# Stick-breaking attention: log-sums over softplus kept per key tile, in two rounded matmul passes

## The chip, the core and the metric

The kernel runs on one core of one Trainium2 chip. The metric is the device time of one execution in microseconds (us). A chip's core has five engines that run side by side, each with its own queue in program order: TensorE (matmuls), VectorE, ScalarE, GpSimd, and SyncE, which issues the DMAs. They wait for one another through semaphores. In profile rows they are PE (PEld for its weight loads), DVE, ACT, POOL and SP.

## The reference

Two transformer-like blocks for 512 tokens of width 1024, in fp32. The first block has two layers, each a gated feed-forward network, a mixing stage, a second feed-forward network and a gated embedding; the second block has one layer with another mixer. The change is in the mixing stage of the first block, which adds up three branches: stick-breaking attention (4 heads of 64), latent attention (8 heads, softmax) and a short gated convolution. For queries t and keys s the stick-breaking branch is

```
z = q @ k.T * 64 ** -0.5                  # mask: s < t
log_not = where(mask, -softplus(z), 0)
after = reverse_cumsum(log_not over s) - log_not
w = where(mask, exp(log_sigmoid(z) + after), 0)
out = w @ v
```

As log_sigmoid(z) = z - softplus(z), the exponent is z minus the sum of softplus over the key itself and all later keys that the query may see.

## The kernel before

Activations lie as [features on 128 partitions, 512 tokens]. Eleven stages follow one another (ffn, mix, ffn, ple, twice; then mix2, ffn, ple). A product with weights is made exact enough by splitting both operands: ScalarE writes a copy rounded to the type F32R (the high part), VectorE subtracts it from the exact value (the low part), and TensorE adds three rounded matmuls (`trio`, L569). TensorE takes a rounded matmul in one pass, and an exact F32 one as two recorded half-passes, each itself two passes. Weights come from HBM by SyncE's DMAs into `raw`, are split by `split_high` (ScalarE, L442) and `split_low` (VectorE, L448), and SyncE issues the DMA of a unit once the low part of the unit two before it is done (L492).

The attention of a mixing stage (`tensor_attention` L961, `scalar_attention` L1551, `vector_attention` L2294) is an order written out by hand on each engine; nothing is reordered at run time. Three strands are woven together: projections of the latent branch; 16 latent steps (`score(t)`, `lat_exp(t)`, `divide(t)`, `turn(t)`, each of two heads and a query tile); and 8 rounds of the stick-breaking branch. A round r covers a pair of heads and one key tile j, from the last tile (3) down to 0, so the queries from tile j on, n = 4 - j tiles of 128 columns. Both heads stand in PSUM banks 4 and 5, which all rounds share. The steps of a round:

- `logits(r)` (TensorE, L1069): z, after the exponential of the round before has left the banks.
- `softplus(r)` (ScalarE, L1602): |z|, exp(-|z|), ln(1 + ...) into `TZ`.
- `masked(r)` (VectorE, L2340): `SP` = max(z, 0) + `TZ`; then the diagonal block is multiplied by the mask; then the diagonal block is copied to the running sum `SS`, if j > 0.
- `after_sum(r)` (TensorE, L1083): adds -1 (lower triangle `ntri`) times `SP` of the own tile, and -1 (`nones`) times `SS`, the running sum of all later tiles, for the queries beyond the own tile. Both are exact F32 matmuls. Then a bf16 matmul adds the mask.
- `weights(r)` (ScalarE, L1606): the exponential out of PSUM.
- GpSimd (L2646 to L2653) adds `SP` to `SS` for the columns beyond the diagonal, after `after_sum(r)`.

`lat_exp(t)` waits for `score_max(t)` on VectorE, `score(t + 1)` on TensorE waits for `lat_exp(t)`, `turn(t)` for `divide(t)`. `keep` (L1611, L2370) brings a finished head pair out of PSUM, again as high and low parts. After `lat_values(3)` the output projection begins (`tensor_last_rows`), with 192 matmuls over 8 units of weights. The first rows of it need the kept pairs.

The tiles of the attention lie in a region of 96 KB, `hid_at`, whose parts are used again and again. `SP` is one [128, 2, 512] tile and `SS` another. The functions that the change touches:

Of the kernel before, what the change touches and what calls it, by code (L numbers as in the profile page):

```python
# [15 lines left out]
P = 128  # L16
# [191 lines left out]
def build_program(nc, a, out):  # L208
    with ExitStack() as ctx:
        def sem(name, step=1):  # L210
            return Signal(ctx.enter_context(nc.semaphore(name)), step)

        cursor = [16 * KB + 128]

# [40 lines left out]
        masks = sb("masks", [P, 3, P], BF16)  # L255
        fw_cols = sb("fw_cols", [P, 4, 2])

        ident = consts[:, 0:P]
# [12 lines left out]
        def hid_tile(name, shape, kb, dt=F32):  # L271
            return at(name, shape, dt, hid_at + kb * KB)
# [21 lines left out]
        SW_FIRST = at("SW_FIRST", [P, 2, DC, T], F32, halves_at)  # L294
        SP = hid_tile("SP", [P, 2, T], 88)
        SS = hid_tile("SS", [P, 2, T], 92)
        PB = [R, RP, U[0], U[1]]
# [663 lines left out]
        def tensor_attention(e, s):  # L961
# [121 lines left out]
            def after_sum(r):  # L1083

                j = key_tile(r)
                rest = slice((j + 1) * P, T)
                e.wait_ge(*vec.at("sb_masked", s, r))
                for h in range(2):
                    e.matmul(ps[4 + h][:, j * P:T], ntri, SP[:, h, j * P:T], start=False, stop=False, skip_group_check=True)  # L1089
                if j < TC - 1:  # L1090
                    e.wait_ge(*(pool if j < TC - 2 else vec).at("sb_running", s, r - 1))
                    for h in range(2):
                        e.matmul(ps[4 + h][:, rest], nones, SS[:, h, rest], start=False, stop=False, skip_group_check=True)  # L1093
                for h in range(2):
# [456 lines left out]
        def scalar_attention(e, s):  # L1551
# [65 lines left out]
            softplus(0)  # L1617
            q_rope(0)
            q_rope(1)
            weights(0)  # L1620
            split_high(e, W[s, "key"])
            softplus(1)
            split_high(e, W[s, "value"])
            q_nope(0)
            weights(1)
            q_nope(1)
            softplus(2)
            key(1)
            key(3)
            lat_exp(0)  # L1630
            weights(2)
# [4 lines left out]
            log_part(3)  # L1636
            lat_exp(2)
            split_high(e, W[s, "out", 0])
            value(2)
# [3 lines left out]
            softplus(4)  # L1643
            value(3)
            lat_exp(5)
            weights(4)
            lat_exp(6)
            softplus(5)
            keep(7, "sb_values", 0, 0)
            lat_exp(7)  # L1650
            keep(6, "lat_values", 0, 2 + 0)
            split_high(e, W[s, "out", 1])
# [3 lines left out]
            softplus(6)  # L1656
            lat_exp(10)
            split_high(e, W[s, "out", 2])
            keep(6, "lat_values", 1, 2 + 1)
# [4 lines left out]
            softplus(7)  # L1664
            lat_exp(14)
            keep(6, "lat_values", 2, 2 + 2)
            lat_exp(15)
# [626 lines left out]
        def vector_attention(e, s):  # L2294
# [45 lines left out]
            def masked(r):  # L2340
                j = key_tile(r)
                diag = slice(j * P, (j + 1) * P)
# [7 lines left out]
                stt(e, SP[:, :, j * P:T], banks[:, 4:6, j * P:T], 0.0, TZ[:, :, j * P:T], ALU.max, ALU.add  # L2350
                    ).then_inc(*vec.done(("sb_softplus", s, r)))
                e.wait_ge(*vec.at("sb_softplus", s, r))
                e.tensor_tensor(SP[:, :, diag], SP[:, :, diag], mask01.unsqueeze(1).to_broadcast([P, 2, P]), ALU.mult
                                ).then_inc(*vec.done(("sb_masked", s, r)))
# [21 lines left out]
            conv_low(1)  # L2376
            masked(0)
            q_rotated(0)
            masked(1)
            split_low(e, W[s, "key"])  # L2380
            q_rotated(1)
            q_cos(0)
# [8 lines left out]
            masked(2)  # L2391
            score_max(0)
            score_max(1)
            divide(0)
# [4 lines left out]
            masked(3)  # L2399
            score_max(3)  # L2400
            divide(2)
            divide(3)
# [3 lines left out]
            masked(4)  # L2406
            turned(3)
            divide(4)
            score_max(6)
# [6 lines left out]
            masked(5)  # L2416
            score_max(8)
            divide(7)
            turned(6)
# [6 lines left out]
            masked(6)  # L2426
            turned(8)
            split_low(e, W[s, "out", 1])
            score_max(11)
# [15 lines left out]
            masked(7)  # L2445
            score_max(15)
            keep(6, 2 + 2)
            turned(14)
# [189 lines left out]
        def gpsimd_mix(e, s):  # L2638
# [6 lines left out]
            e.tensor_tensor(CS[:, 3, :], CS[:, 3, :], CS[:, 4, :], ALU.add).then_inc(*pool.done(("kv_squares", s)))  # L2645
            for r in range(ROUNDS):  # L2646
                j = key_tile(r)
# [129 lines left out]
```

## Time and profile before

| | us |
|---|---|
| median of 3 runs | 2835.51 (2834.59 to 2835.59) |
| span of the profiled execution | 2832.4 |
| around the span, by the median | 3.1 |
| TensorE busy | 2824.2 (100%), 14154 matmul records |
| VectorE busy | 1554.6 (55%), 2272 instructions |
| ScalarE busy | 1163.4 (41%), 1816 instructions |
| GpSimd busy | 36.6 (1%), 38 instructions |

The profiled execution's time is given as its span, from the first to the last instruction; the 3.1 us beside it are the difference to the median of the runs. Busy time is the union of an engine's records. Matmuls are pipelined and their ends are modelled, so records overlap and TensorE counts as busy where it only finishes; the distance between the starts of neighbours is the better price of a matmul. The clock granted to TensorE is full in every slice of the span.

### The profile page before, as it was taken

To read this page: it belongs to the slowest core of one execution; us is meant where nothing else is said; L and a number is where in the kernel's file an instruction comes from. 1 tells how busy PE (TensorE), PEld (TensorE's weight loads), DVE (VectorE), ACT (ScalarE), POOL (GpSimd) and SP (SyncE) were. 2 spreads that over 40 slices of the span, in tenths; PEclk is the share of its full clock that TensorE was granted. 3 is DMA by queue.
4 is the path that set the end of the run, shared out by engine and by line. 5 is a ranking of instruction groups with operands and counts; after the bars stand their busy time and mean duration, and the time that the engine had idled before them with its cause. 6 is when DMAs were issued, how large, how long until landed. Compare 5 with 4: busy or idle time off the path is not lost.

```text
span 2832.4 us, 35135 instructions
## 1 busy us (share of the span) xinstructions
PE 2824.2 (100%) x14154; PEld 2357.8 (83%) x14154; DVE 1554.6 (55%) x2272; ACT 1163.4 (41%) x1816; POOL 36.6 (1%) x38
## 2 busy tenths in 40 slices
PE   9999999999999999999999999999999999999999
PEld 7888887698888898888976788888987889888888
DVE  5443466755442585442566564433776756766437
ACT  5332344553332563332535543323754545322235
POOL 0000000000000000000000000000001100000000
PEclk9999999999999999999999999999999999999999
DMA  5333323033333223333232223333232323333331
GB/s 161 98 97 101 124 56 95 17 97 112 97 97 97 82 90 104 97 97 97 76 105 53 90 81 97 98 97 120 68 101 82 96 78 102 101 101 97 104 119 60
DMA packets 200657, 264.93 MB, mean 94 GB/s; under 512 B 34992, under 2 KB 153136, under 8 KB 200496
## 3 DMA queue, kind: packets, MB, share of 16 engines
q1 hardware_dynamic: 200352, 262.68, 30.4%
q8 instruction: 113, 1.85, 0.3%
q14 instruction: 48, 0.39, 0.0%
q10 hardware_dynamic: 144, 0.00, 0.0%
HBM read 258.44 MB, written 2.10 MB: 92 GB/s over the span
## 4 chain that ended last, share of the span: by engine, by line
PE 98%; DVE 1%; ACT 0%; issue 0%; DMA 0%; SPq 0%; DVEq 0%; ACTq 0%
PE banks L570 31%; PE banks L571 31%; PE banks L572 31%; PE banks L1030 1%; PE banks L1052 1%; PE banks L1089 1%; PE banks L1041 1%; PE banks L1093 0%; PE banks L1079 0%; PE banks L609 0%; PE banks L1183 0%; DVE PT L2366 0%; PE banks L1012 0%; PE banks L976 0%; PE banks L1014 0%
## 5 line engine op out<-in xcount | busy, mean ns | idle before, releaser
L570 PE MATMUL banks<-HH,WH 128*128 128x512 f32 (+1 forms) x3132 | 1140.1, 364 | 0.3 <-DVE HL L1790 0.3
L571 PE MATMUL banks<-HH,WL 128*128 128x512 f32 (+1 forms) x3132 | 1135.2, 362 | 0.0
L572 PE MATMUL banks<-HL,WH 128*128 128x512 f32 (+1 forms) x3132 | 1135.0, 362 | 0.0
L451 DVE TENSOR_TENSOR WL<-raw,WH 128x1024 fp32r<-128x1024 f32 (+1 forms) x482 | 581.5, 1209 | 981.4 <-ACT WH L446 981.0
L446 ACT ACTIVATE WH<-raw 128x1024 fp32r<-128x1024 f32 (+1 forms) x482 | 501.8, 1044 | 1012.0 <-PE banks L572 799.4
L570 PEld LDWEIGHTS banks<-HH,WH 128*128 128x128 f32 x3132 | 591.2, 189 | 100.7 <-issue 6.9
L572 PEld LDWEIGHTS banks<-HL,WH 128*128 128x128 f32 x3132 | 591.3, 189 | 91.9
L571 PEld LDWEIGHTS banks<-HH,WL 128*128 128x128 f32 x3132 | 591.4, 189 | 91.1 <-issue 1.0
L570 PE MATMUL banks<-HIDH,WH 128*128 128x512 f32 (+1 forms) x1056 | 377.7, 358 | 0.0
L572 PE MATMUL banks<-HIDL,WH 128*128 128x512 f32 (+1 forms) x1056 | 376.8, 357 | 0.0
L571 PE MATMUL banks<-HIDH,WL 128*128 128x512 f32 (+1 forms) x1056 | 376.8, 357 | 0.0
L571 PEld LDWEIGHTS banks<-HIDH,WL 128*128 128x128 f32 x1056 | 199.5, 189 | 29.2
L572 PEld LDWEIGHTS banks<-HIDL,WH 128*128 128x128 f32 x1056 | 199.5, 189 | 28.8
L570 PEld LDWEIGHTS banks<-HIDH,WH 128*128 128x128 f32 x1056 | 199.5, 189 | 28.7
L1427 ACT ACTIVATE HIDH<-U 128x512 fp32r<-128x512 f32 x112 | 69.3, 634 | 106.1 <-DVE U L2015 106.1
L1284 ACT ACTIVATE HH<-X,par 128x256 fp32r<-128x256 f32 x160 | 72.8, 502 | 85.5 <-DVE X L1910 85.5
L1423 ACT ACTIVATE G<-G 128x512 f32<-128x512 f32 x88 | 55.7, 632 | 124.3 <-DVE G L1982 124.3
L1982 DVE TENSOR_TENSOR U<-banks,R 128x512 f32<-128x512 f32 x112 | 76.6, 684 | 27.5 <-ACT G L1423 26.6
L1982 DVE TENSOR_TENSOR G<-banks,R 128x512 f32<-128x512 f32 x112 | 76.8, 686 | 18.1 <-PE banks L572 18.1
L1890 DVE TENSOR_TENSOR U<-U,SQY 128x256 f32<-128x256 f32 x120 | 50.8, 423 | 65.4 <-ACT SQY L1267 63.6
L2020 DVE TENSOR_TENSOR HIDL<-U,HIDH 128x512 fp32r<-128x512 f32 x112 | 72.6, 690 | 5.5
L1790 DVE SCALAR_TENSOR_TENSOR HL<-X,par,HH 128x256 fp32r<-128x256 f32 x160 | 70.0, 480 | 0.6 <-ACT HH L1284 0.6
(272 smaller groups left out, 1967.1 us busy)
## 6 DMA issues: line engine op xcount, KB each, us to landing
raw<-in_w_up SPq DMA_DIRECT2D x264, 256.0 KB, 3.1
raw<-in_w_down SPq DMA_DIRECT2D x112, 512.0 KB, 3.5
raw<-in_w_gate SPq DMA_DIRECT2D x168, 256.0 KB, 2.8
raw<-in_w_in SPq DMA_DIRECT2D x68, 512.0 KB, 3.7
raw<-in_w_ple_gate SPq DMA_DIRECT2D x24, 512.0 KB, 3.6
raw<-in_w_out SPq DMA_DIRECT2D x16, 512.0 KB, 3.8
raw<-in_w_rg_out SPq DMA_DIRECT2D x8, 512.0 KB, 3.5
raw<-in_w_o SPq DMA_DIRECT2D x8, 512.0 KB, 3.5
```

Source lines behind the costliest of these rows:

```text
L446: e.activation(WH[tile_of[u]][:, 0:n], raw[raw_of(u)][:, 0:n], ACT.Copy).then_inc(*high.done((u,)))
L451: e.tensor_tensor(WL[tile_of[u]][:, 0:n], raw[raw_of(u)][:, 0:n], WH[tile_of[u]][:, 0:n].bitcast(F32), ALU.subtract).then_inc(*low.done((u,)))
L570: e.matmul(o, wh, ah, start=start, stop=False, skip_group_check=skip)
L571: e.matmul(o, wl, ah, start=False, stop=False, skip_group_check=skip)
L572: return e.matmul(o, wh, al, start=False, stop=stop, skip_group_check=skip)
L1284: e.activation(HH[:, n, part(h)], X[:, n, part(h)], ACT.Copy, scale=pre_gain(s, n)).then_inc(*act.done(("h_high", s, h, n)))
L1423: e.activation(G[j][:], G[j][:], ACT.Silu).then_inc(*act.done(("gate", s, g, j)))
L1427: e.activation(HIDH[:, 2 * g + j, :], U[j][:], ACT.Copy).then_inc(*act.done(("hidden_high", s, 2 * g + j)))
L1790: return e.scalar_tensor_tensor(out=o, in0=in0, scalar=scalar, in1=in1, op0=op0, op1=op1)
L1890: e.tensor_tensor(TOTAL_Y[h], TOTAL_Y[h], SQY[y_place[s, h, n] % 2][:], ALU.add).then_inc(*vec.done(("y_sum", s, h, n)))
L1982: return e.tensor_tensor(o, ps[bank][:], R[:], ALU.mult).then_inc(*vec.done(event))
L2020: e.tensor_tensor(HIDL[:, k, :], U[j][:], HIDH[:, k, :].bitcast(F32), ALU.subtract).then_inc(*vec.done(("hidden_low", s, k)))
```

## The change

The softplus of each key tile is kept in a tile of its own until the pair of heads is done, split into a rounded high part `SPH[j]` (ScalarE, `sums_high`) and a rounded low part `SPL[j]` (VectorE, `sums_low`, in place of `SP[j]`). TensorE sums over tiles: for every tile later than j it adds `round_nones` times high and low, and for the own tile `round_ntri` times high and low. The running sum `SS`, its copy on VectorE, the additions on GpSimd and the waits for them are gone. Two 128x128 constants are rounded once at the start by ScalarE. The tiles are placed anew: the allocation begins 15 KB lower, and the scratch area for dynamic DMAs is set to 1 KB.

```diff
-        cursor = [16 * KB + 128]
+        cursor = [KB + 128]
...
+        round_nones = sb("round_nones", [P, P], F32R)
+        round_ntri = at("round_ntri", [P, P], F32R, consts_at + 4 * 6 * P)
+        SPH = [sb(f"SPH{j}", [P, 2, (TC - j) * P], F32R) for j in range(TC)]
+        widest_sp = take(4 * KB)
...
-        SP = hid_tile("SP", [P, 2, T], 88)
-        SS = hid_tile("SS", [P, 2, T], 92)
+        sp_at = [widest_sp, hid_at + 91 * KB, hid_at + 89 * KB, hid_at + 88 * KB]
+        SP = [at(f"SP{j}", [P, 2, (TC - j) * P], F32, sp_at[j]) for j in range(TC)]
+        SPL = [at(f"SPL{j}", [P, 2, (TC - j) * P], F32R, sp_at[j]) for j in range(TC)]
...
             def after_sum(r):
                 j = key_tile(r)
-                rest = slice((j + 1) * P, T)
-                e.wait_ge(*vec.at("sb_masked", s, r))
+                if r == 0:
+                    e.wait_ge(*act.at("round_sums", 1))
+                e.wait_ge(*vec.at("sb_softplus", s, r))
+                for earlier in range(TC - 1, j, -1):
+                    for h in range(2):
+                        for half in (SPH, SPL):
+                            e.matmul(ps[4 + h][:, earlier * P:T], round_nones[:], half[earlier][:, h, :], start=False,
+                                     stop=False, skip_group_check=True)
+                e.wait_ge(*vec.at("sb_low", s, r))
                 for h in range(2):
-                    e.matmul(ps[4 + h][:, j * P:T], ntri, SP[:, h, j * P:T], start=False, stop=False, skip_group_check=True)
-                if j < TC - 1:
-                    e.wait_ge(*(pool if j < TC - 2 else vec).at("sb_running", s, r - 1))
-                    for h in range(2):
-                        e.matmul(ps[4 + h][:, rest], nones, SS[:, h, rest], start=False, stop=False, skip_group_check=True)
+                    for half in (SPH, SPL):
+                        e.matmul(ps[4 + h][:, j * P:T], round_ntri[:], half[j][:, h, :], start=False, stop=False,
+                                 skip_group_check=True)
...
+            for i, (rounded, exact) in enumerate(((round_ntri, ntri), (round_nones, nones))):
+                e.activation(rounded[:], exact, ACT.Copy).then_inc(*act.done(("round_sums", i)))
...
+            def sums_high(r):
+                j = key_tile(r)
+                e.wait_ge(*vec.at("sb_masked", s, r))
+                e.activation(SPH[j][:], SP[j][:], ACT.Copy).then_inc(*act.done(("sb_high", s, r)))
...
             def masked(r):
...
-                    if key_tile(r - 1) > 0:
-                        e.wait_ge(*vec.at("sb_running", s, r - 1))
-                    if 0 < key_tile(r - 1) < TC - 1:
-                        e.wait_ge(*pool.at("sb_running", s, r - 1))
...
-                if j > 0:
-                    e.wait_ge(*vec.at("sb_masked", s, r))
-                    e.tensor_copy(SS[:, :, diag], SP[:, :, diag]).then_inc(*vec.done(("sb_running", s, r)))
+            def sums_low(r):
+                j = key_tile(r)
+                e.wait_ge(*act.at("sb_high", s, r))
+                e.tensor_tensor(SPL[j][:], SP[j][:], SPH[j][:].bitcast(F32), ALU.subtract).then_inc(*vec.done(
+                    ("sb_low", s, r)))
...
-                if 0 < j < TC - 1:
-                    rest = slice((j + 1) * P, T)
-                    e.wait_ge(*vec.at("sb_running", s, r))
-                    e.wait_ge(*pe.at("sb_sum", s, r))
-                    e.tensor_tensor(SS[:, :, rest], SS[:, :, rest], SP[:, :, rest], ALU.add
-                                    ).then_inc(*pool.done(("sb_running", s, r)))
```

The new calls stand in the written orders as follows. On ScalarE: `sums_high(0)` between `q_rope(0)` and `q_rope(1)`; (1) after `split_high` of "value", before `q_nope(0)`; (2) after `key(3)`, before `lat_exp(0)`; (3) after `lat_exp(2)`, before the split of output unit 0; (4) after `value(3)`, before `lat_exp(5)`; (5) after `lat_exp(7)`, before `keep(6, ...)`, the split of output unit 1 and `lat_exp(8)`; (6) after `lat_exp(10)`, before the split of output unit 2; (7) after `lat_exp(14)`, before `keep(6, ...)` and `lat_exp(15)`. On VectorE: `sums_low(0)` after `masked(0)`; (1) after the split of "key"; (2) after `score_max(0)`; (3) after `score_max(3)`, before `divide(2)`; (4) after `turned(3)`, before `divide(4)`; (5) after `score_max(8)`, before `divide(7)`; (6) after `turned(8)`, before the split of output unit 1 and `score_max(11)`; (7) after `score_max(15)`, before `keep(6, ...)`, `turned(14)` and `divide(15)`.

## Rows read from the trace of the kernel before

**Rows 1.** The page: busy us (share of the span) xinstructions of each engine.

```profile
PE 2824.2 (100%) x14154; PEld 2357.8 (83%) x14154; DVE 1554.6 (55%) x2272; ACT 1163.4 (41%) x1816; POOL 36.6 (1%) x38
```

**Rows 2.** Windows: us, then busy us (xinstructions) of each engine, clock, DMA.

```profile
468.20:561.70 93.50, 92.00 (x484) 58.96 (x482) 68.37 (x144) 57.51 (x123) 4.01 (x4) 1.00 0.14 39
533.20:547.20 14.00, 13.29 (x73) 7.86 (x70) 13.60 (x33) 9.05 (x22) 1.27 (x1) 1.00 0.13 39
```

**Rows 3.** Timeline of TensorE, start us then duration: rounded matmuls, first and last of a run.

```profile
401.06 0.39 PE L570 MATMUL banks<-HH,WH 128*128 128x512 f32 x1
...
404.91 0.39 PE L572 MATMUL banks<-HL,WH 128*128 128x512 f32 x1
...
583.68 0.28 PE L571 MATMUL banks<-HH,WL 128*128 128x256 f32 x1
...
588.12 0.28 PE L572 MATMUL banks<-HL,WH 128*128 128x256 f32 x1
...
2826.22 0.27 PE L571 MATMUL banks<-HH,WL 128*128 128x128 f32 x1
...
2828.68 0.28 PE L572 MATMUL banks<-HL,WH 128*128 128x128 f32 x1
```

**Rows 4.** Timeline of TensorE: the sums of rounds 1, 2 and 3.

```profile
484.27 1.02 PE L1089 MATMUL banks<-SP,consts 128*128 128x256 f32 x4
...
485.58 0.28 PE L1095 MATMUL banks<-masks 128*128 128x128 bf16 x2
...
494.53 1.51 PE L1089 MATMUL banks<-SP,consts 128*128 128x384 f32 x4
...
496.74 0.28 PE L1095 MATMUL banks<-masks 128*128 128x128 bf16 x2
...
507.38 1.94 PE L1089 MATMUL banks<-SP,consts 128*128 128x512 f32 x4
...
510.44 0.28 PE L1095 MATMUL banks<-masks 128*128 128x128 bf16 x2
```

**Rows 5.** Timeline: the mask of round 2, a weight split on ScalarE.

```profile
493.55 0.42 DVE L2353 TENSOR_TENSOR SP<-SP,consts 128x256 f32<-128x256 f32 x1
...
504.43 1.05 ACT L446 ACTIVATE WH<-raw 128x1024 fp32r<-128x1024 f32 x1
```

**Rows 6.** Timeline of VectorE: the score maximum of latent step 3.

```profile
507.58 1.23 DVE L2328 TENSOR_REDUCE stats<-banks 128x2 f32<-128x1024 f32 x1 [1.16 <-PE banks L1031]
```

**Rows 7.** Timeline, round 4: exponential of step 5, mask, score of step 6.

```profile
515.36 0.47 ACT L1585 ACTIVATE U<-banks,stats 128x256 f32<-128x256 f32 x1 [1.01 <-DVE stats L2328]
...
515.69 0.42 DVE L2353 TENSOR_TENSOR SP<-SP,consts 128x256 f32<-128x256 f32 x1
...
516.83 0.91 PE L1030 MATMUL banks<-KM,QM 96*128 96x384 f32 x2
```

**Rows 8.** Timeline, round 5: kept copy, mask, exponential of step 8, score of step 9.

```profile
525.78 0.59 ACT L1613 ACTIVATE HH<-banks 128x512 fp32r<-128x512 f32 x1
...
526.17 0.42 DVE L2353 TENSOR_TENSOR SP<-SP,consts 128x256 f32<-128x256 f32 x1
...
527.36 0.37 ACT L1585 ACTIVATE R<-banks,stats 128x128 f32<-128x128 f32 x1
...
528.18 0.65 PE L1030 MATMUL banks<-KM,QM 96*128 96x256 f32 x2
```

**Rows 9.** Timeline of VectorE, round 6: mask, weight split, score maximum of step 11.

```profile
535.03 0.43 DVE L2353 TENSOR_TENSOR SP<-SP,consts 128x256 f32<-128x256 f32 x1
...
536.10 1.22 DVE L451 TENSOR_TENSOR WL<-raw,WH 128x1024 fp32r<-128x1024 f32 x1
...
537.47 1.23 DVE L2328 TENSOR_REDUCE stats<-banks 128x2 f32<-128x1024 f32 x1 [0.15 <-PE banks L1031]
```

**Rows 10.** Timeline, the end of round 7: last division, last turn.

```profile
555.10 0.17 DVE L2334 RECIPROCAL stats<-stats 128x2 f32<-128x2 f32 x1
...
555.94 1.04 PE L1041 MATMUL banks<-consts,U 128*128 128x128 f32 x8
```

More of the change, by code:

```diff
@@ L1618, in scalar_attention @@
             q_rope(0)
+            sums_high(0)
             q_rope(1)
@@ L1623, in scalar_attention @@
             split_high(e, W[s, "value"])
+            sums_high(1)
             q_nope(0)
@@ L1629, in scalar_attention @@
             key(3)
+            sums_high(2)
             lat_exp(0)
@@ L1637, in scalar_attention @@
             lat_exp(2)
+            sums_high(3)
             split_high(e, W[s, "out", 0])
@@ L1644, in scalar_attention @@
             value(3)
+            sums_high(4)
             lat_exp(5)
@@ L1650, in scalar_attention @@
             lat_exp(7)
+            sums_high(5)
             keep(6, "lat_values", 0, 2 + 0)
@@ L1657, in scalar_attention @@
             lat_exp(10)
+            sums_high(6)
             split_high(e, W[s, "out", 2])
@@ L1665, in scalar_attention @@
             lat_exp(14)
+            sums_high(7)
             keep(6, "lat_values", 2, 2 + 2)
@@ L2341, in masked @@
                 j = key_tile(r)
-                diag = slice(j * P, (j + 1) * P)
                 e.wait_ge(*act.at("sb_log", s, r))
@@ L2345, in masked @@
                     e.wait_ge(*pe.at("sb_sum", s, r - 1))
-                    if key_tile(r - 1) > 0:
-                        e.wait_ge(*vec.at("sb_running", s, r - 1))
-                    if 0 < key_tile(r - 1) < TC - 1:
-                        e.wait_ge(*pool.at("sb_running", s, r - 1))
-                stt(e, SP[:, :, j * P:T], banks[:, 4:6, j * P:T], 0.0, TZ[:, :, j * P:T], ALU.max, ALU.add
+                stt(e, SP[j][:], banks[:, 4:6, j * P:T], 0.0, TZ[:, :, j * P:T], ALU.max, ALU.add
                     ).then_inc(*vec.done(("sb_softplus", s, r)))
                 e.wait_ge(*vec.at("sb_softplus", s, r))
-                e.tensor_tensor(SP[:, :, diag], SP[:, :, diag], mask01.unsqueeze(1).to_broadcast([P, 2, P]), ALU.mult
-                                ).then_inc(*vec.done(("sb_masked", s, r)))
-                if j > 0:
-                    e.wait_ge(*vec.at("sb_masked", s, r))
-                    e.tensor_copy(SS[:, :, diag], SP[:, :, diag]).then_inc(*vec.done(("sb_running", s, r)))
+                e.tensor_tensor(SP[j][:, :, 0:P], SP[j][:, :, 0:P], mask01.unsqueeze(1).to_broadcast([P, 2, P]),
+                                ALU.mult).then_inc(*vec.done(("sb_masked", s, r)))
+            def sums_low(r):
[3 more added lines that the diff above has]
+                    ("sb_low", s, r)))
             def turned(t):
@@ L2377, in vector_attention @@
             masked(0)
+            sums_low(0)
             q_rotated(0)
@@ L2380, in vector_attention @@
             split_low(e, W[s, "key"])
+            sums_low(1)
             q_rotated(1)
@@ L2392, in vector_attention @@
             score_max(0)
+            sums_low(2)
             score_max(1)
@@ L2400, in vector_attention @@
             score_max(3)
+            sums_low(3)
             divide(2)
@@ L2407, in vector_attention @@
             turned(3)
+            sums_low(4)
             divide(4)
@@ L2417, in vector_attention @@
             score_max(8)
+            sums_low(5)
             divide(7)
@@ L2427, in vector_attention @@
             turned(8)
+            sums_low(6)
             split_low(e, W[s, "out", 1])
@@ L2446, in vector_attention @@
             score_max(15)
+            sums_low(7)
             keep(6, 2 + 2)
@@ L2645, in gpsimd_mix @@
             e.tensor_tensor(CS[:, 3, :], CS[:, 3, :], CS[:, 4, :], ALU.add).then_inc(*pool.done(("kv_squares", s)))
-            for r in range(ROUNDS):
-                j = key_tile(r)
-                if 0 < j < TC - 1:
-                    rest = slice((j + 1) * P, T)
-                    e.wait_ge(*vec.at("sb_running", s, r))
-                    e.wait_ge(*pe.at("sb_sum", s, r))
-                    e.tensor_tensor(SS[:, :, rest], SS[:, :, rest], SP[:, :, rest], ALU.add
-                                    ).then_inc(*pool.done(("sb_running", s, r)))
         def gpsimd_mix2(e, s):
@@ L2766 @@
     from concourse.bass_utils import run_bass_kernel_spmd
-    nc = bacc.Bacc("TRN2", target_bir_lowering=False, num_devices=1)
+    nc = bacc.Bacc("TRN2", target_bir_lowering=False, num_devices=1, dynamic_dma_scratch_size=KB)
     arrays, aps = {}, {}
```

## The prediction

> **What bounds the kernel now.** I read the busy line first: TensorE is busy for 2824.2 of 2832.4 us [rows 1], and nearly the whole chain of waits lies on it too. No other engine is near it over the whole span, so an edit pays if it shortens TensorE's own queue and costs if it makes TensorE wait. Next I read the stretch of the change, the attention of the two mixing stages. In the first, 468.2 to 561.7 us, TensorE is busy 92.00 of 93.50 us, VectorE 68.37, ScalarE 57.51 [rows 2]; the second repeats it 1024.95 us later instruction by instruction, so I work out one and double it. The average of VectorE, 73%, hides parts where it is dense. Last, I walked the order of events of the three engines around each of the eight rounds. A round is named by the number n of query tiles that it covers: rounds 0 to 3 and 4 to 7 have n = 1 to 4.
>
> **What TensorE saves.** Matmuls overlap in the records, so the price of one is the distance between starts. Rounded matmuls start 0.112 us apart at 128 columns (22 steps in 2.46 us), 0.120 at 256 (37 steps in 4.44) and 0.2265 at 512 (17 steps in 3.85) [rows 3]; for 384 I take the middle, 0.173. An exact sum is recorded as two half-passes, each twice as long as its columns. Before, the sums of a round took 1.31 us for n = 2 (484.27 to 485.58), 2.21 for n = 3 (494.53 to 496.74) and 3.06 for n = 4 (507.38 to 510.44) [rows 4]. After, a round has four rounded matmuls of each width from 128 to its own (two heads, high and low): n = 2: 4 x 0.112 + 4 x 0.120 = 0.93; n = 3: 0.93 + 4 x 0.173 = 1.62; n = 4: 1.62 + 4 x 0.2265 = 2.53. A round with n = 1 has four narrow records before and four narrow matmuls after: nothing. Saved: 0.38 + 0.59 + 0.53 = 1.50 us for four rounds, 3.0 for a stage, 6.0 for the kernel. A narrow matmul costs twice what its columns do, so the sums per tile, three of 128 columns where one running sum stood, eat about half of what halving the passes would give.
>
> The Trainium skill, TensorE: Matmul & The Clock Gate, section Back-to-back issue gap, gives about 81 ns as the sustained spacing at 128 columns. The trace has 112 ns for these fp32 weights [rows 3], so the measurement decides; by 81 ns the 64 narrow matmuls would together be 2.0 us cheaper.
>
> **What the new steps cost.** Before, the sum waited for softplus and mask on VectorE. Now the mask is followed by a copy on ScalarE (high part), then by a subtraction on VectorE (low part), and only then by the sum over the own tile; the sums over earlier tiles need softplus alone. The like operations are the splits of weights: 1.05 us for a 1024-wide rounded copy on ScalarE, 1.22 for the subtraction on VectorE [rows 5, 9]. For narrower ones I draw a line to 0.47 us on ScalarE and 0.42 on VectorE at 256 [rows 7, 8]: copy 0.47, 0.66, 0.86, 1.05 and subtraction 0.42, 0.69, 0.96, 1.22 for n = 1 to 4. The running-sum copy on VectorE goes, six times a stage, and the additions on GpSimd; a copy costs no more than the mask of the same size, 0.42 [rows 8], and I take half of that, 0.2. Queue order is what matters: whoever stands behind a waiting copy or subtraction waits too. The walk, with "late" meaning against the trace of before:
>
> Rounds 0 and 1: high and low are ready over 1 us before TensorE comes. TensorE is 0.38 early after round 1, but the next step of VectorE is dense up to the mask of round 2, which stays where it is, ending 493.97 [rows 5].
>
> Round 2 (n = 3): high 494.85, low 495.84. TensorE, there at 494.15, has the earlier sums done at 495.08, stalls 0.8, and ends the round at 496.6 against 496.74. Early by 0.15.
>
> Round 3 (n = 4): the high part is ready in good time, but the subtraction stands behind the score maximum (507.58 to 508.81 before, [rows 6]; 0.15 early now), so low ends at 508.66 + 1.22 - 0.08 = 509.80, where 0.08 is the overlap of two operations that don't wait for each other. TensorE starts at 507.23, ends the earlier sums at 508.85, stalls 1.0, ends at 510.75 against 510.44. Late by 0.31.
>
> Round 4 (n = 1): the copy is put ahead of the exponential of latent step 5, which began at 515.36; the mask ended later, at 516.11 [rows 7]. So the exponential begins at about 516.9, its first head ends near 517.5, and the score matmul of step 6, which began at 516.83 and was due at 517.14, waits. Late by 0.71.
>
> Round 5 (n = 2): mask ended 526.59, now 527.30; high 527.99; then come a kept copy and a weight split (1.58 us of queue, 525.78 to 527.36), so the exponential of step 8 starts at 529.49 against 527.36 [rows 8]. The score of step 9, at 528.18 before, had 0.31 us of slack: late by 1.82. The own stall of the sum (0.9 for the low part, done at 528.7) lies inside it.
>
> Round 6 (n = 3): TensorE finds its low part ready, but VectorE has waited for the high part and subtracted ahead of a weight split and the next score maximum. The mask ended at 535.46, now 537.28; with 0.03 us from one engine to the next the high part is done at 538.17, the low part at 539.16, the split, 1.22 less 0.08, at 540.30, and the score maximum goes from 537.47 [rows 9] to 540.22: late by 2.75. From 533.2 to 547.2 us VectorE is busy for 13.60 of 14.00 us [rows 2] and TensorE waits on it, so 2.75 is passed on whole.
>
> Round 7 (n = 4): the low part (1.22, less 0.08 overlap) stands ahead of a kept subtraction, a turned copy and the last division, which began at 555.10 with nothing to spare [rows 10]. Its result is 2.75 + 1.14 = 3.89 late; the last turn on TensorE (555.94) had 0.2 of slack, and 0.35 more is won back because the stick-breaking values no longer wait for their exponential. Late by 3.35 at the end of the stage.
>
> The output rows that follow are one unbroken run of matmuls, and nothing there gives time back. The output weights have cover: a unit lasts some 5.4 us on TensorE (24 x 0.2265) and its split, with the weight DMA that SyncE issues behind it, comes at most 3.9 late. If that cover were gone it would cost up to 3.9 a stage. The two 128x128 copies at the start (some 0.25 each in ScalarE's queue) I cost at nothing, as the matmuls of the first group run beside them; uncovered they are 0.5 us in all. No row shows other addresses in SBUF or the smaller scratch area. The nearest are the two stages, which differ by nothing that I can see, and I take 0, with 1 us either way. A wait set between the two parts of a sum costs nothing if the signal is there; the extreme is a refill of the first load, 0.2 a round, 3 us in all. GpSimd's 4.01 us a stage [rows 2] lie beside everything: 0.
>
> **Sum.** 2 x 3.35 = 6.7 us on the profiled 2832.4. The runs give a median of 2835.51, which is 3.1 above the span for what lies around it; I predict 2835.5 + 6.7 = 2842.2.
>
> **The rivals.**
> (a) Saving without waits: every high and low part is ready in time, since the mean load of VectorE leaves 25 us a stage. The whole 6.0 comes in: 2829.5. Rounds 0, 1, 4 and 6 speak for it, the positions of copy and subtraction in rounds 3, 5 and 7 against it.
> (b) Only the direct stalls count (0.8 + 1.0 + 0.9 + 0.3 = 3.0 a stage) and what stands behind the copies is absorbed by idle time further on. They equal the 3.0 saved: 2835.5. The gaps of ScalarE speak for it; that the latent scores wait on each exponential speaks against it.
> (c) VectorE becomes the bound of the whole attention: eight subtractions are 2 x (0.42 + 0.69 + 0.96 + 1.22) = 6.6 us a stage, less 6 x 0.2 for the copies that go, 5.4. Then it costs 10.8: 2846.3. It decides from the point where VectorE has no idle left between rounds; it is so from 533 to 547 us, while over the whole stage it is idle for 25 us [rows 2].
> The Trainium skill, same page, section Architectural detail, has ScalarE and VectorE as strict FIFO. This gives no number of its own, but by that rule nothing can pass a waiting copy, and the trace agrees in that the exponentials keep the program's order.
> That the rounded passes don't run as single ones I give no chance: these are the kernel's own operand kinds, with the spacing of [rows 3].
>
> **How the numbers follow.** Forecast 0.45, (a) 0.13, (b) 0.22, (c) 0.20. The forecast's own range is 2839 to 2846: 1.5 us a stage for slack misread by a few tenths in eight rounds. For 8 in 10 I reach from (a) to somewhat past (c): 2830 to 2848. 0.2%, about what a measurement of this kernel can tell from no change, is 5.7 us, so slower is above 2841.2: two thirds of the forecast and nearly all of (c), 0.50. Faster, below 2829.8, is most of (a), 0.12. The rest, 0.38, is the same.
>
> **What would show it.** Sums of n = 4 on TensorE: 2.53 us of matmuls with a gap of 1.0 before the own tile in round 3. The exponential of step 8 2.1 us late against 527.36. The score maximum of step 11 2.7 late. The stage from its first query matmul to the first output row 96.9 us against 93.5, twice. I am wrong if a low part is ready before TensorE has summed the earlier tiles in rounds 3 and 7, or if TensorE's idle time in the attention grows by less than its sums shrink.

## The result, and the profile after

The changed kernel takes 2841.42 us (median of 9 runs, 2840.97 to 2842.64) against 2834.87 for the kernel before on the same chip (9 runs, 2834.09 to 2835.59): ratio 1.0024, 95% interval 1.0014 to 1.0034, 6.5 us slower. The profiled spans differ by 6.8 us, 2839.2 against 2832.4.

The page of the kernel after, busy line and shares of the chain of waits that ended last:

```profile
PE 2821.7 (99%) x14202; PEld 2360.9 (83%) x14202; DVE 1562.7 (55%) x2276; ACT 1173.3 (41%) x1834; POOL 28.6 (1%) x30
PE 96%; DVE 2%; issue 1%; ACT 1%; DMA 0%; SPq 0%; ACTq 0%
```

TensorE is busy 2.5 us less than in [rows 1] although the span is 6.8 longer: it stands idle some 9 us more. Windows of the first attention and of its dense part, columns as in [rows 2]:

```profile
468.20:564.90 96.70, 91.02 (x507) 60.04 (x506) 72.56 (x146) 62.46 (x131) 0.00 (x0) 1.00 0.13 38
533.20:547.20 14.00, 12.73 (x78) 7.75 (x75) 13.31 (x30) 8.87 (x20) 0.00 (x0) 1.00 0.13 39
```

The window is 96.70 us long, where 93.50 stood in [rows 2]; counted from the stage's own first matmul, which comes 0.17 us earlier here, the stage takes 96.8. VectorE has 4.2 us more work in it, ScalarE 5.0. The table of waits of TensorE (who waited for whom: us in total, times, longest):

```profile
PE banks L1102 <- DVE SPL L2379: 4.4, 8, 0.8
PE banks L1035 <- ACT U L1597: 2.0, 4, 0.8
PE banks L1046 <- DVE U L2362: 1.6, 2, 0.8
```

L1102 are the own tile's sums, L1035 the latent scores, L1046 the turns. None of the three is in the table of the kernel before. In the timelines that follow a line is start us, us, engine; the whole trace after runs 0.17 us earlier up to the attention, so 0.17 is added when a start is set against one of before.

Round 3, answering to [rows 4, 6]:

```profile
507.13 0.31 PE L1097 MATMUL banks<-SPH,round_nones 128*128 128x128 f32 x1
...
508.50 1.22 DVE L2379 TENSOR_TENSOR SPL<-SP,SPH 128x1024 fp32r<-128x1024 f32 x1
...
508.67 0.34 PE L1097 MATMUL banks<-SPL,round_nones 128*128 128x384 f32 x1
...
509.78 0.50 PE L1102 MATMUL banks<-SPH,round_ntri 128*128 128x512 f32 x1 [0.77 <-DVE SPL L2379]
...
510.81 0.29 PE L1105 MATMUL banks<-masks 128*128 128x128 bf16 x2
```

The last of the earlier sums starts at 508.67 and takes 0.17, so they end at 508.84, and the own sums start at 509.78: the gap is 0.94, and 3.68 us in all stand where 3.06 did. Round 5, answering to [rows 8]:

```profile
527.24 0.63 ACT L1621 ACTIVATE SPH<-SP 128x512 fp32r<-128x512 f32 x1 [0.75 <-DVE SP L2373]
...
527.51 0.42 DVE L2353 TENSOR_REDUCE stats<-banks 128x2 f32<-128x256 f32 x1 [0.31 <-PE banks L1036]
...
527.78 0.58 ACT L1630 ACTIVATE HH<-banks 128x512 fp32r<-128x512 f32 x1
528.25 1.05 ACT L451 ACTIVATE WH<-raw 128x1024 fp32r<-128x1024 f32 x1
...
529.20 0.36 ACT L1597 ACTIVATE R<-banks,stats 128x128 f32<-128x128 f32 x1
529.70 0.48 PE L1035 MATMUL banks<-KM,QM 96*128 96x256 f32 x1 [0.19 <-ACT R L1597]
```

Here the queue is seen at work. The high part waits for the mask, and the kept copy and the weight split, which could have gone earlier, stand behind it. The exponential of step 8 has its maximum at 527.93 (527.51 + 0.42), when the high part is done, but stands behind the copy and the split until 529.20: 1.27 us in the queue. Round 6, answering to [rows 9], and the end of the stage, answering to [rows 10]:

```profile
537.95 0.96 DVE L2379 TENSOR_TENSOR SPL<-SP,SPH 128x768 fp32r<-128x768 f32 x1 [0.51 <-ACT SPH L1621]
...
538.82 1.22 DVE L456 TENSOR_TENSOR WL<-raw,WH 128x1024 fp32r<-128x1024 f32 x1
...
539.96 1.22 DVE L2353 TENSOR_REDUCE stats<-banks 128x2 f32<-128x1024 f32 x1
...
542.04 0.38 PE L1035 MATMUL banks<-KM,QM 96*128 96x128 f32 x1 [0.85 <-ACT U L1597]
...
558.61 0.15 DVE L2359 RECIPROCAL stats<-stats 128x2 f32<-128x2 f32 x1
...
559.34 1.09 PE L1046 MATMUL banks<-consts,U 128*128 128x128 f32 x8 [0.79 <-DVE U L2362]
...
564.82 0.50 PE L575 MATMUL banks<-HH,WH 128*128 128x512 f32 x1
```

### The profile page after: what moved, and what is told of

It is laid out like the page before. It is cut to its first block, busy times and chain, and to the rows that moved or that the text cites. A ratio compares the mean times of both kernels' runs of the same rounds, so it can differ in the third digit from the quotient of the medians.

```text
span 2839.2 us, 35233 instructions
## 1 busy us (share of the span) xinstructions
PE 2821.7 (99%) x14202; PEld 2360.9 (83%) x14202; DVE 1562.7 (55%) x2276; ACT 1173.3 (41%) x1834; POOL 28.6 (1%) x30
## 4 chain that ended last, share of the span: by engine, by line
PE 96%; DVE 2%; issue 1%; ACT 1%; DMA 0%; SPq 0%; ACTq 0%
PE banks L575 31%; PE banks L576 31%; PE banks L577 31%; PE banks L1035 1%; PE banks L1057 1%; PE banks L1046 0%; PE banks L614 0%; PE banks L1193 0%; DVE stats L2353 0%; PE banks L1084 0%; DVE SP L1815 0%; DVE PT L2389 0%; PE banks L1102 0%; DVE SPL L2379 0%; DVE QM L2341 0%
```

## The experiments

Theory: the price is paid in the written orders of ScalarE and VectorE, where latent steps stand behind the new copies and subtractions. Rivals: only TensorE's direct waits for the low parts; VectorE's load as such; the new addresses.

Each time is the median of 8 to 11 runs and is compared with runs of the kernel before made beside them (2834.28 to 2834.57 us). Beside the time I use one number from each profile, the **stage length**, from the start of the first score matmul to the start of the first output row (first and second stage). It is 67.84 and 67.83 us before, 71.56 and 71.40 after, and what comes ahead of the stage doesn't disturb it. Ahead of it the changed kernel has won 0.4 us in rounds 0 and 1 (493.26 + 0.17 against 493.84).

**layout**: the kernel before with the new base address and scratch area.

```diff
-        cursor = [16 * KB + 128]
+        cursor = [KB + 128]
```
and `dynamic_dma_scratch_size=KB`.

> The kernel before, with only the new addresses (allocation 15 KB lower, 1 KB of scratch). Theory (addresses cost nothing): the time of before, 2834.9, within 1 us. Rival (part of the slowdown comes from the addresses): up to the measured 6.5 us above it.

Measured: 2834.22, ratio 1.0001 [0.9992, 1.0010], stage 67.85 and 67.84. The shift of the addresses and the smaller scratch area cost nothing; the tiles of their own for each key tile are not in this kernel.

**nosplit**: the sums without the two split operations. Softplus and mask write one rounded tile per key tile, and both passes of a sum read it; the low part is left out, so this kernel and those built on it compute another result.

```diff
-            sums_high(0)   # and (1) to (7)
-            sums_low(0)    # and (1) to (7)
...
-                        for half in (SPH, SPL):
+                        for half in (SP, SP):
```

> The changed kernel without any high and low parts: softplus and mask write one rounded tile, and every sum reads that tile twice. This leaves out the copy and the subtraction and so computes another result; TensorE's matmuls are those of the changed kernel in number and size. Theory (the sums are worth 3.0 us a stage when nothing has to be waited for): 6.0 below before, and up to 2 us more as the six running-sum copies on VectorE are gone too: 2827 to 2829. Rival (the narrow matmuls cost more than they save): 2834 or more.

Measured: 2831.10, ratio 0.9988 [0.9980, 0.9997], stage 66.57 and 66.56. Expected was 2827 to 2829. Even with no wait for a split and no split in a queue only 3.2 of the 6.0 us come in: a miss, followed up below. Part of it is the 6.0 itself. Here nothing interrupts the sums, and the eight rounds of the first stage take 11.52 us from the first sum to the mask matmul, against 14.04 before: TensorE sheds 2.5 us a stage, 5.0 for the kernel, and not 6.0.

**nowait**: the split operations in their places, but no sum waits for them.

```diff
-                e.wait_ge(*vec.at("sb_low", s, r))
+                e.wait_ge(*vec.at("sb_masked", s, r))
```

> As the kernel without parts, but the copy on ScalarE and the subtraction on VectorE are made at their places in the queues; the sums don't wait for them and read the one rounded tile twice (another result). Theory (most of the cost comes from what stands behind them in the queues): direct waits go (about 2.3 us in all), queue costs stay: 2839, range 2837.5 to 2840. Rival b (only the direct stalls cost): 2829, as without the parts.

Measured: 2839.0, ratio 1.0017 [1.0008, 1.0026], stage 70.40 and 70.36. Between this kernel and nosplit lie only the split operations in two queues: 7.9 us. Between it and the kernel after lie the direct waits: 4.7 against 6.5 us above the runs of before beside each, so 1.8. Four of the eleven runs of nowait have a mean granted clock of 0.999 and take 2839.9 to 2840.6 us, the seven at 1.000 take 2837.7 to 2839.2, so the two shares are good to about half a microsecond; by the stage lengths, from profiles at full clock, they are 7.6 and 2.2. ScalarE's line is the one of round 5 above. The wait for the low part is gone (0.72 us there), and TensorE waits longer for the exponential instead (1.11 for 0.19; timeline of nowait):

```profile
528.02 1.05 ACT L450 ACTIVATE WH<-raw 128x1024 fp32r<-128x1024 f32 x1
528.96 0.36 ACT L1596 ACTIVATE R<-banks,stats 128x128 f32<-128x128 f32 x1
...
529.46 0.70 PE L1034 MATMUL banks<-KM,QM 96*128 96x256 f32 x2 [1.11 <-ACT R L1596]
```

**out6**: the split of output unit 1 on VectorE, and of unit 3 on ScalarE, moved behind the last latent steps.

```diff
-            split_high(e, W[s, "out", 3])
             keep(6, "lat_values", 3, 2 + 3)
             keep(7, "sb_values", 1, 1)
+            split_high(e, W[s, "out", 3])
...
             sums_low(6)
-            split_low(e, W[s, "out", 1])
             score_max(11)
...
             turned(15)
+            split_low(e, W[s, "out", 1])
```

> The changed kernel with the split of output unit 1 on VectorE moved from round 6 to behind the last turned copy, and ScalarE's split of unit 3 behind the last two kept copies. Theory (VectorE is the bound from round 6 to round 7, so 1.14 us less in its queue there comes off each stage): 2.3 below the changed kernel's 2841.4, 2839.1. Rival (the exponential chain, not VectorE's load, sets that stretch): 0.9 a stage at the score of step 12 and nothing later, under 0.5 in all.

Measured: 2838.81, ratio 1.0016 [1.0007, 1.0025], stage 70.49 and 70.68. It stands 4.5 us above the runs of before beside it, where the kernel after stands 6.5 above its own: 2.0 less, for 2.3 expected. In the first stage the wait of 0.85 at step 12 is gone. Held.

**order_all**: out6, and in rounds 4, 5 and 7 latent steps ahead of what they had been put behind. On VectorE the mask of round 5 also goes ahead of the split of unit 0 and, the other way round, its subtraction ahead of the score maximum of step 8.

```diff
-            sums_high(4)
             lat_exp(5)
+            sums_high(4)
...
             sums_high(5)
-            keep(6, "lat_values", 0, 2 + 0)
-            split_high(e, W[s, "out", 1])
             lat_exp(8)
+            keep(6, "lat_values", 0, 2 + 0)
             weights(5)
+            split_high(e, W[s, "out", 1])
...
-            split_low(e, W[s, "out", 0])
             masked(5)
-            score_max(8)
+            split_low(e, W[s, "out", 0])
             sums_low(5)
+            score_max(8)
...
             sums_low(7)
-            keep(6, 2 + 2)
             turned(14)
             divide(15)
+            keep(6, 2 + 2)
```

> The changed kernel with five things moved in the written orders and nothing else: the copy of round 4 behind the exponential of step 5; the exponential of step 8 ahead of the kept copy and weight split of round 5; the mask of round 5 ahead of the split of output unit 0 on VectorE; the split of output unit 1 behind the last turned copy; the kept subtraction of round 7 behind the last division. By the walk a stage gets back 0.35 (round 4), 0.95 (round 5), 0.9 (round 6), 0.6 (round 7): 2.8, so 5.6 for the kernel, and it ends within 1.5 us of the kernel before (2833.5 to 2836.5 where before is 2834.9). Rival (the copies and subtractions cost by their work, wherever they stand): 2838 or more.

Measured: 2835.65, ratio 1.0004 [0.9995, 1.0012], stage 68.83 twice. The same instructions in another order give back 5.4 us (1.1 above before instead of 6.5), and 2.6 to 2.7 a stage in length. Round 5 on ScalarE in order_all:

```profile
526.22 0.63 ACT L1621 ACTIVATE SPH<-SP 128x512 fp32r<-128x512 f32 x1
...
528.01 0.37 ACT L1597 ACTIVATE R<-banks,stats 128x128 f32<-128x128 f32 x1 [1.16 <-DVE stats L2353]
```

The exponential goes at 528.01 instead of 529.20, and what it waits for is its own maximum. Of the three new lines of TensorE's table the wait for the exponentials is gone, the one for the division is down to 0.4 us, and the own sums of rounds 2, 3 and 7 are left:

```profile
PE banks L1102 <- DVE SPL L2379: 3.1, 6, 0.8
```

**before_out6** and **nosplit_out6**: the move of out6 in the kernel before and in nosplit.

> The kernel before with the same move of the split of unit 1. Theory (VectorE was already the bound of that stretch before the change): 0.3 to 0.9 us a stage, 0.6 to 1.8 below before. Rival (only the changed kernel is bound by VectorE there): no difference, within 0.3.

> The kernel without high and low parts (another result, as told for it) with the split of unit 1 moved out of round 6. It gained 3.2 of the 6.0 us by which TensorE's sums shrink. Theory (the rest was lost because VectorE bounds rounds 6 and 7): about 1 us a stage more, 5 to 6 below before. Rival (TensorE's sums shrank by less than the spacing says): no more than 0.5 beyond the 3.2.

Measured: 2834.61 (1.0000 [0.9991, 1.0008]) and 2830.87 (0.9988 [0.9979, 0.9997]); the stages are 67.85 and 66.57, as without the move. Unburdening VectorE's dense stretch is worth 0.7 to 1.1 us a stage where subtractions stand in it and nothing where they don't. The theory that this load swallowed the rest of nosplit's saving fell.

**swap6**: the score maximum of step 11 ahead of the split that stands in its way, both still in round 6.

```diff
             sums_low(6)
+            score_max(11)
             split_low(e, W[s, "out", 1])
-            score_max(11)
```

> The changed kernel with the split of unit 1 merely put behind the score maximum of step 11, still in round 6. The score maximum comes about 0.9 us earlier. Theory (VectorE's load, not that one wait, sets the stretch): under 0.4 us a stage comes in, 2840.6 or more where the changed kernel has 2841.4. Rival (the late exponential of step 11 is what costs): 0.9 a stage, 2839.6.

Measured: 2842.30, ratio 1.0027 [1.0017, 1.0037]. No gain, as expected, and the trace shows where it went (timeline of swap6, where like events come 0.01 us later than in the trace after up to here):

```profile
541.14 0.49 PE L1035 MATMUL banks<-KM,QM 96*128 96x128 f32 x2
...
541.33 0.16 DVE L2359 RECIPROCAL stats<-stats 128x2 f32<-128x2 f32 x1
...
543.35 0.52 PE L1046 MATMUL banks<-consts,R 128*128 128x128 f32 x3 [0.98 <-DVE PT L2389]
```

The score of step 12 starts at 541.14 instead of 542.04, but the split now holds up the next division (541.33, where the kernel after has 541.09) and with it a copy that the next turn waits for: the turn starts at 543.35, where the kernel after has 543.11. The stages are 73.08 and 71.54. The second is no shorter than in the kernel after; the first is longer by a stretch at a lower clock, of which the last section tells.

**nosplit_half** and its control **before_half**. In nosplit, TensorE reaches step 12 earlier and finds its exponential not done (timeline of nosplit):

```profile
535.76 0.22 PE L1035 MATMUL banks<-masks 128*128 128x128 bf16 x1
536.01 1.23 DVE L2344 TENSOR_REDUCE stats<-banks 128x2 f32<-128x1024 f32 x1 [0.48 <-PE banks L1035]
...
537.27 0.69 ACT L1596 ACTIVATE U<-banks,stats 128x512 f32<-128x512 f32 x1 [1.89 <-DVE stats L2344]
...
537.96 0.68 ACT L1596 ACTIVATE U<-banks,stats 128x512 f32<-128x512 f32 x1
...
538.77 0.30 PEld L1034 LDWEIGHTS banks<-KM,QM 96*128 96x128 f32 x2 [0.35 <-ACT U L1596]
```

Neither VectorE nor ScalarE is late here: both were idle. From the last mask of one score to the second head of the next, 3.01 us pass in hops, and the sums between have become shorter than that. So both kernels got a shorter chain. The maximum that is subtracted ahead of the exponential is taken over the first half of a score row only; that is another shift of the softmax:

```diff
-                e.tensor_reduce(out=stats[:, c:c + 2], in_=banks[:, 0:2, 0:w], axis=AXX, ...
+                e.tensor_reduce(out=stats[:, c:c + 2], in_=banks[:, 0:2, 0:w // 2], axis=AXX, ...
```

> The kernel nosplit (2831.1 us, the two split operations left out), with score_max reducing only the first half of each score row (1.23 us become about 0.69 at 512 keys, 0.96 become about 0.56 at 384, 0.69 become 0.43 at 256): the softmax is shifted by another maximum and the rest of the work is the same. What it tells: where the 2.8 us of TensorE's 6.0 went that nosplit did not show. Theory: the chain score, score_max on VectorE, lat_exp on ScalarE, next score has a fixed length, and with less of the sums between two scores TensorE comes to its end; shortened by 0.5 us it gives back what it swallowed, so 2828.2 to 2830.0, the first output row of the first stage 0.6 to 1.3 earlier than nosplit's 559.8. Rival: the rest is lost elsewhere (division, turns, copies of blocks): within 0.5 of nosplit, 2830.6 to 2831.6.

> The control: the kernel before with the same half-width score_max. Theory: in the kernel before TensorE's own work is longer than the chain (0.48 us of slack at the twelfth score), so nothing is gained: 2834.0 to 2834.6. Rival: the chain held the kernel before as well, or VectorE's time does: 1.0 to 2.8 faster, 2831.7 to 2833.5.

Measured: 2827.67 (0.9976 [0.9966, 0.9986], stage 64.80 twice) and 2833.32 (0.9995 [0.9986, 1.0004], stage 67.26 and 67.23). The first gained 3.4 us, somewhat more than expected; the control gained 1.2 where I had said none, so the chain already cost the kernel before a little. Against each other, in runs made side by side, they stand 2833.32 - 2827.67 = 5.65 us apart, where the same two kernels with whole maxima stand 3.18 apart: with a shorter chain 2.5 us more come in. The 5.65 are not the sums alone. These shrink by 5.1 in this pair; the other 0.5 or so must come from what went with the running sum (six copies a stage on VectorE, GpSimd's additions), which no run takes apart. A narrower maximum also takes work off VectorE; that it is the length of the chain that counts is shown by head_max below, which puts work on VectorE and gains all the same. The same place in nosplit_half, where the row of step 12 has no wait left:

```profile
535.52 0.69 DVE L2344 TENSOR_REDUCE stats<-banks 128x2 f32<-128x512 f32 x1 [0.72 <-PE banks L1035]
...
537.85 0.44 PE L1034 MATMUL banks<-KM,QM 96*128 96x128 f32 x2
```

**high_first**: order_all with the own sums of both high parts ahead of the wait for the low part.

```diff
-                e.wait_ge(*vec.at("sb_low", s, r))
-                for h in range(2):
-                    for half in (SPH, SPL):
+                e.wait_ge(*act.at("sb_high", s, r))
+                for half in (SPH, SPL):
+                    if half is SPL:
+                        e.wait_ge(*vec.at("sb_low", s, r))
+                    for h in range(2):
```

> The kernel order_all (2835.65 us), with the own tile's four rounded matmuls in another order: both heads of the high part first, as soon as ScalarE's copy is there, then both heads of the low part behind the wait for VectorE's subtraction. Same work, same result up to the order of adding. Theory: the wait of 0.64 in round 2 and 0.77 in round 3 is a wait for the low part alone, and 0.35 and 0.45 us of high matmuls fit into it, 0.17 in round 7 and less elsewhere: 0.8 to 1.0 a stage, 1.6 to 2.0 in all: 2833.5 to 2834.3, the waits of own sums from 3.1 to 1.3 to 1.6 in total. It would then be level with or 0.3 ahead of the kernel before (2834.5). Rival: the wait only moves, because the weights and the next softplus start at the same time as the low part is finished plus its matmuls, and the latent chain sets the pace anyway: under 0.5 faster, 2835.1 to 2835.7.

Measured: 2834.49, ratio 0.9999 [0.9990, 1.0008], stage 67.98 and 68.13. It gains 1.2, between the two expectations (1.6 to 2.0, and under 0.5). The wait for low parts fell from 3.1 to 0.9 in the table, but part of it came back as a wait for the last division (1.3 in all, 0.4 in order_all).

**head_max**: high_first with the score maximum of wide steps taken head by head, nothing left out. TensorE signals each head's score, and each exponential waits for its own head's maximum. The cut shows VectorE's part.

```diff
...
+                for h in range(2):
+                    e.wait_ge(*(pe.at("score", s, t) if h else pe.at("score", s, t, 0)))
+                    e.tensor_reduce(out=stats[:, c + h:c + h + 1], in_=banks[:, h, 0:w], axis=AXX, op=ALU.max,
+                                    negate=True).then_inc(*vec.done(("score_max", s, t) if h else ("score_max", s, t, 0)))
```

> The kernel high_first (2834.5 us), with the score maximum of steps of 384 and 512 keys taken head by head: the first head's reduction (about 0.56 and 0.69 us) can start behind the first head's mask, and ScalarE's first exponential starts behind it, where both waited for one reduction over both heads (0.96 and 1.23). Nothing is left out; VectorE gets eight more instructions a stage, about 0.12 to 0.16 each. Theory: after the direct waits, the chain score, maximum, exponential, next score is what swallows TensorE's saving, and it is 0.5 to 0.7 shorter at a wide step; half-width maxima gave 3.4 to the kernel without split operations and 1.25 to the kernel before, with 0.3 to 0.5 less work each on VectorE, which this doesn't give: 1.0 to 2.0 faster, 2832.5 to 2833.5, the wait for the exponential of step 11 at the second head of step 12 (0.35) gone, and then 0.4 to 0.7 per thousand ahead of the kernel before. Rival: what half-width maxima gave was VectorE's time and not the length of the chain; eight more instructions a stage then cost it about 1.2 a stage of queue: 2834.5 to 2836.

Measured: 2832.17 (11 runs), ratio 0.9992 [0.9983, 1.0001], stage 66.69 and 66.68: 2.2 us better than high_first when each is set against the runs of before beside it, a little more than expected, and that with eight more instructions a stage on VectorE. Its row at step 11:

```profile
536.78 1.28 DVE L2361 TENSOR_REDUCE stats<-banks 128x1 f32<-128x512 f32 x2
...
537.50 0.69 ACT L1599 ACTIVATE U<-banks,stats 128x512 f32<-128x512 f32 x1 [0.20 <-DVE stats L2361]
```

Both reductions together take 1.28 us, but the exponential starts 0.72 after the first begins, where nosplit needed 1.26. This is the fastest kernel that leaves nothing out: 2.3 us under the kernel before, with an interval that just touches 1. It doesn't show that the split sums are worth 2.3, as the kernel before with its maxima taken head by head was not run; half-width maxima alone gave that kernel 1.2.

## Why the prediction was right

The median came out 6.5 us up for 6.7 predicted, and the steps, not only the sum, mostly hold:

- **TensorE's sums.** Round 1: 0.92 (484.06 to 484.98 in the trace after) for 0.93. Own sums of n = 4: 1.03 for 0.91, the 0.12 being the longer first spacing after a wait (509.78 to 510.11). Without any wait, in nosplit, n = 3 takes 1.70 for 1.62 and n = 4 2.65 for 2.53: the first matmul of a sum and the first of 256 columns are each followed some 0.05 later than the even spacing says (507.13 to 507.28 for 0.11, 507.62 to 507.79 for 0.12). The prediction also took its exact sums from rounds 1 to 3, and those of rounds 5 to 7 differ a little (1.37, 2.15 and 3.01 us). So the 6.0 was a misjudged size: 5.0.
- **Rounds 2 and 3.** Gap before the own sums of round 3: 0.94 for 1.0. Round 2 ended 0.04 early for 0.15, and round 3 0.54 late for 0.31, as the sums are the longer ones just named.
- **Round 4.** Score of step 6 late by 517.45 + 0.17 - 516.83 = 0.79 for 0.71.
- **Round 5.** Exponential of step 8 late by 529.20 + 0.17 - 527.36 = 2.01 for 2.13; score of step 9 by 1.69 for 1.82.
- **Round 6.** Score maximum of step 11 late by 2.66 for 2.75.
- **Round 7.** Last division late by 3.68 for 3.89; first output row by 564.82 + 0.17 - 561.68 = 3.31 for 3.35. The stage measured 96.8 for 96.9.

The errors are 0.1 to 0.2 us each way, and some of them cancel: that the end came within 0.04 is partly luck, that it came within a few tenths is not.

Rival (c), VectorE's load as a whole, is refuted: with all its subtractions in place order_all loses 0.4 per thousand, not 10.8 us. Rival (b) fell with nowait, which keeps most of the loss without a single direct wait. Rival (a) was wrong even in its premise: in nosplit, where nothing waits for a split, only 3.2 us came in.

One part of the working was wrong without harm to the forecast. I treated the 3.0 a stage as time that is saved wherever nothing stalls; rivals (a) and (b) rest on it. The forecast's own sum, 2 x 3.35, doesn't: it follows the times of events, and from round 4 on TensorE waits for the queues, which are later than any saving. The step that a change to the order would have shown wrong is "Saved: ... 6.0 for the kernel". TensorE's work shrinks by 5.0, and of that only 3.2 are time as long as scores, maxima and exponentials form a chain of fixed length. Taken apart by the runs, the result is -3.2 (sums) + 7.9 (queue places) + 1.8 (direct waits) = 6.5. The prediction's reason for the smaller saving is also put wrongly: the sums per tile of n = 4 are not three of 128 columns but one each of 128, 256 and 384 (rows of round 3 above), so each pass takes 768 columns where the running sum had 384, and at n = 4 these added columns eat more (by the spacing at 512 columns an estimated 0.7 us a round) than the narrow matmuls' price does (0.25).

The Trainium skill bears on two of the terms. VectorE: DVE Perf Modes, section The TRN2 errata, gives (N + 151) / 0.96 ns for an fp32 tensor_tensor over N elements; the trace agrees to 0.01: 0.42, 0.69, 0.96 and 1.22 us at 256, 512, 768 and 1024 elements for the low parts. TensorE: Matmul & The Clock Gate, section LDWEIGHTS (loading the stationary operand), has the load as columns / 1.2 ns, which would make about 107 ns an estimate of the least spacing of matmuls with 128-column weights. The narrow sums are 0.11 us apart (484.12, 484.23, 484.34), so as a spacing that figure fits these rows where the 81 ns quoted in the prediction doesn't; as the duration of a load it doesn't fit, since the load records of these sums last 0.19 us.

## What to carry to other kernels

An operation that waits also holds up what stands behind it in its queue: here 16 operations a stage, 32 in all, cost 7.9 us by their places in the queues and 1.8 by direct waits, 9.7 above nosplit; with the steps on which the next engine waits put first in most places, the same operations cost 4.3. Before counting matmul time as saved, find the cross-engine chain between the same two matmuls and compare: what TensorE sheds below that length is not time. A reduction split so that the next engine can start on its first half shortens the chain even though it is more work. Where a product has parts that become ready at different times, issue the ready part ahead of the wait.

## What the runs showed of the hardware that I had not expected

In 8 of the 14 profiles one of the stages, in head_max both, begins with a wait of 0.2 to 1.0 us at the first latent score for the DMA that turns the queries; in the kernel after it is in the second stage:

```profile
1522.11 0.49 PE L1035 MATMUL banks<-KM,QM 96*128 96x128 f32 x2 [0.70 <-DMA QM<-QR]
```

It occurs in kernels with the old sums too (1.02 us in layout, 0.64 in before_half, none in before and before_out6), which issue the same DMAs, so it is no effect of the change. How much of the spread between runs it makes is not shown. It is why the stage length, in which the two stages of a profile agree to 0.04 us in most kernels and to 0.2 in all but swap6, told more than one profile's span.

A short fall of TensorE's clock is seen in one profile, the first stage of swap6. Windows, columns as in [rows 2]:

```profile
546.00:547.00 1.00, 1.00 (x7) 1.00 (x6) 0.97 (x3) 0.00 (x0) 0.00 (x0) 0.50 0.00 0
547.00:548.00 1.00, 1.00 (x7) 0.67 (x5) 0.70 (x2) 0.57 (x2) 0.00 (x0) 0.50 0.00 0
```

The granted clock is 0.50, the lower of the two levels (1.2 for 2.4 GHz), from about 545.2 to 548.6 us; ahead of it TensorE had stood idle 0.98 us (until 543.35) and 0.28 us (until 544.47). That stage is 1.5 us longer than the other. Five of swap6's eight runs have a mean clock of 0.999 and take 2842.2 to 2844.1 us; the three at 1.000 take 2841.1 to 2841.6, which is the time of the kernel after. Part of the spread between runs is thus the clock. That the idle stretches brought the clock down is not shown; in the profile of the kernel after TensorE idles 0.85 us at the same place (542.04) and the clock stays at 1.00.

A rounded matmul that starts after a wait is followed at 0.28 to 0.34 us by the next instead of 0.17 to 0.23 (495.72 to 496.00 at 384 columns, 509.78 to 510.11 at 512): such a wait in the middle of a sum costs TensorE another 0.11 us beyond the idle time that the table names. The longer spacing belongs to the break and not to the wait itself: it is there behind a bf16 matmul with no wait too (485.08 to 485.39 at 512 columns), and it is not there where the own sums follow the earlier ones at once (540.21 to 540.38 at 384).
